# Down products placed between the second-half gate and up products in seven of eleven feed-forward blocks

## What is computed

```
def _swiglu(x, w_in, w_out):
    gate, up = jnp.split(x @ w_in, 2, axis=-1)
    return (jax.nn.silu(gate) * up) @ w_out

x = _layernorm(DEEPNORM_ALPHA * x + FFN_RESIDUAL * _swiglu(x, ffn_w_in[i, f], ffn_w_out[i, f]), ...)
```

## Time and profile before

| what | value |
|---|---|
| time, median of 3 runs | 1402.48 us (1402.14 to 1402.58) |
| the profiled execution | 1402.65 us |
| its span, first to last instruction | 1400.8 us |
| PE busy | 1388.0 us (99%) |
| DVE busy | 1090.6 us (78%) |
| ACT busy | 695.7 us (50%) |
| POOL busy | 61.4 us (4%) |

### The profile page before, as it was taken

The page is one execution under the profiler, slowest core; times in us unless marked ns, Lnnn a source line. Parts: engine busy times, 40 slices in busy tenths (PEclk is TensorE's granted clock), DMA queues, the critical chain, the costliest instruction groups (busy, mean ns, idle before and its releaser), DMA issues.

```text
span 1400.8 us, 21435 instructions
## 1 busy us (share of the span) xinstructions
PE 1388.0 (99%) x8920; PEld 1248.0 (89%) x8920; DVE 1090.6 (78%) x1416; ACT 695.7 (50%) x907; POOL 61.4 (4%) x116
## 2 busy tenths in 40 slices
PE   9999999999999999999999999999999999999997
PEld 8888889999999888888888888899999998888886
DVE  6766687889888986667976667868998889766687
ACT  5544445674546454444454444457646464544442
POOL 0600000000000110000000000000000001000000
PEclk9999999999999999999999999999999999999998
DMA  9765545547654686555566555555466447665541
GB/s 299 248 216 183 197 158 170 188 146 234 205 151 153 199 267 202 180 181 180 181 211 219 190 191 181 180 180 167 154 227 181 151 157 241 213 198 197 189 150 60
DMA packets 169280, 265.31 MB, mean 189 GB/s; under 512 B 9294, under 2 KB 102048, under 8 KB 169184
## 3 DMA queue, kind: packets, MB, share of 16 engines
q1 hardware_dynamic: 163936, 249.53, 54.0%
q0 software_dynamic: 5104, 14.29, 3.5%
q10 hardware_dynamic: 144, 0.13, 0.0%
HBM read 260.51 MB, written 1.05 MB: 187 GB/s over the span
## 4 chain that ended last, share of the span: by engine, by line
PE 97%; DVE 2%; DMA 0%; SPq 0%; ACT 0%; issue 0%; DVEq 0%
PE ps L1593 21%; PE ps L1416 19%; PE ps L1418 19%; PE ps L1417 19%; PE ps L1595 11%; PE ps L1453 4%; PE ps L1715 2%; PE ps L1560 1%; DMA raw<-in_ffn_w_in 0%; DVE big L953 0%; DVE wlo L864 0%; PE ps L1828 0%; DVE xtok L958 0%; PE ps L1576 0%; PE ps L1808 0%; DVE big L988 0%
## 5 line engine op out<-in xcount | busy, mean ns | idle before, releaser
L864 DVE TENSOR_TENSOR wlo<-raw,whi 128x1024 fp32r<-128x1024 f32 x468 | 549.0, 1220 | 159.8 <-ACT whi L587 159.6
L587 ACT CAST whi<-raw 128x1024 fp32r<-128x1024 f32 x460 | 458.8, 1049 | 369.5 <-PE ps L1418 229.9
L1593 PE MATMUL ps<-xhl,whi 128*128 128x512 f32 x1280 | 446.2, 392 | 0.0
L1595 PE MATMUL ps<-xhl,wlo 128*128 128x256 f32 x1280 | 357.9, 280 | 0.0
L1416 PE MATMUL ps<-xhl,whi 128*128 128x256 f32 x1056 | 298.5, 283 | 0.0
L1418 PE MATMUL ps<-xhl,wlo 128*128 128x256 f32 x1056 | 296.3, 281 | 0.0
L1417 PE MATMUL ps<-xhl,whi 128*128 128x256 f32 x1056 | 296.2, 281 | 0.0
L1593 PEld LDWEIGHTS ps<-xhl,whi 128*128 128x128 f32 x1280 | 240.2, 188 | 52.9
L1595 PEld LDWEIGHTS ps<-xhl,wlo 128*128 128x128 f32 x1280 | 240.5, 188 | 1.4
L1416 PEld LDWEIGHTS ps<-xhl,whi 128*128 128x128 f32 x1056 | 199.1, 189 | 2.0 <-issue 1.8
L1417 PEld LDWEIGHTS ps<-xhl,whi 128*128 128x128 f32 x1056 | 199.1, 189 | 0.1
(11 more groups left out here) (267 smaller groups left out, 1430.9 us busy)
## 6 DMA issues: line engine op xcount, KB each, us to landing
raw<-in_ffn_w_in SPq DMA_DIRECT2D x170, 512.0 KB, 5.0
raw<-in_w_in SPq DMA_DIRECT2D x140, 512.0 KB, 4.5
raw<-in_ffn_w_out SPq DMA_DIRECT2D x88, 512.0 KB, 4.1
raw<-in_w_br SPq DMA_DIRECT2D x32, 512.0 KB, 5.0
raw<-in_w_out SPq DMA_DIRECT2D x16, 512.0 KB, 4.6
raw<-in_ple_gate_w SPq DMA_DIRECT2D x16, 512.0 KB, 4.6
gv<-in_ln_g POOLq DMA_DIRECT2D x8, 512.0 KB, 4.5
b_bc<-in_ln_b POOLq DMA_DIRECT2D x8, 512.0 KB, 6.3
```

The source lines that it names most:

```text
L587: nc.scalar.copy(whi[:, slot, half_], raw[:, source, half_]).then_inc(whi_half, 1)
L864: ins = nc.vector.tensor_tensor(low, source_, high.bitcast(F32), ALU.subtract)
L1593: nc.tensor.matmul(ps[:, 2 * q + u, :], w[:, k, u, P * q:P * q + P], xhl[:, :, 4 * kk + k, :], start=kk == 0 and k == 0, stop=False, skip_ ...
L1595: ins = nc.tensor.matmul(ps[:, 2 * q + u, 256:512], v[:, k, u, P * q:P * q + P], xh[:, 4 * kk + k, :], start=False, stop=kk == 1 and k == ...
```

## The change

For j = 2 to 8, `gate_up(j)` also issues the 24 down matmuls of block j-1. They stand in kk = 1: behind each of the last 12 of its 16 pairs come two of them (`down_steps`), in the same order as before. The separate `down(j-1)` calls behind the block fall away. The signals `gate0_done` and `chunk_used` of the block are sent by the last pair of q = 0 and of q = 1, ahead of the two down matmuls that follow there. The first down matmul now waits for `hlo_made` and for its chunk behind the fifth pair of kk = 1.

On ACT and DVE, in the same seven blocks, the cast and the low part of chunk g+5 (= 3j+4, the down chunk of the next step) move from behind `hhi` and `hlo` to between: on ACT ahead of the silu of q = 1, on DVE between `sums` and product of q = 1. No arithmetic and no transfer is added or removed.

```
@@ ACT, ffn @@
+                    woven = 2 <= j < NFF - 2
...
                     else:
+                        if woven:
+                            his(g + RING + 2)
                         act.wait_ge(gsum_made, 2 * (n - n0 // NFF))
                         nc.scalar.activation(sil[:, 1, :], gsum[:, 1, :], ACT.Silu).then_inc(silu_made, 1)
@@ DVE, ffn @@
                             sums(n, q, g)
+                            if q == 1 and 2 <= j < NFF - 2:
+                                los(g + RING + 2)
                             product_of_sums(n, q)
@@ PE, ffn @@
-                def gate_up(j):
+                def gate_up(j, woven=None):
...
+                                    if woven is None or kk == 0:
+                                        continue
+                                    if q == 0 and u == 1 and k == 3:
+                                        ins.then_inc(gate0_done, 1)
+                                    if q == 1 and u == 1 and k == 3:
+                                        ins.then_inc(chunk_used, 1)
+                                    if 8 * q + 4 * u + k >= 4:
+                                        down_steps(woven, 2 * (8 * q + 4 * u + k - 4), 2)
-                            if kk == 1 and q == 0:
+                            if kk == 1 and q == 0 and woven is None:
                                 ins.then_inc(gate0_done, 1)
-                        ins.then_inc(chunk_used, 1)
+                        if woven is None or kk == 0:
+                            ins.then_inc(chunk_used, 1)
...
+                def down_steps(j, first, count):
+                    c = c0 + wo_at(j)
+                    if first == 0:
+                        pe.wait_ge(hlo_made, n0 + j + 1)
+                        chunk_ready(c)
+                    w, v = weights(c, 2, D)
+                    hi, lo = hhi[j % HIDS], hlo[j % HIDS]
+                    for i in range(first, first + count):
+                        t, cg, k, kind = i // 12, i // 6 % 2, i // 3 % 2, i % 3
+                        ins = nc.tensor.matmul(ps[:, 4 + 2 * t + cg, :], (hi, hi, lo)[kind][:, k, P * t:P * t + P],
+                                               (w, v, w)[kind][:, k, W * cg:W * cg + W], start=False, stop=False,
+                                               skip_group_check=True)
+                        if i == 23:
+                            ins.then_inc(chunk_used, 1)
...
                 for j in range(2, NFF - 2):
-                    gate_up(j)
-                    for t in range(TT):
-                        down(j - 1, t)
+                    gate_up(j, woven=j - 1)
```

## The result

The changed kernel takes 1405.39 us (median of 18 runs, 1404.64 to 1405.60) against 1402.50 (18 runs, 1402.13 to 1403.20): a ratio of 1.0020, 95% interval 1.0014 to 1.0027. It is 2.9 us slower. That is 0.01 us within the upper end of the range (1405.4) and just past the line that the forecast drew at 0.2% (1405.3), beyond which it would call the kernel slower, with a chance of 0.14. The single figure of 1403.2 was 2.2 us too low.

What follows compares the result with a forecast made beforehand. The prediction took PE's pace to bound the kernel. Its terms, -0.8 + 0.9 + 0.6 = +0.7 us on the profiled 1402.65, gave 1403.2 against a median of 1402.48; the range was 1400.6 to 1405.4.

Steps and rivals of the forecast that it cites:

- What bounds the kernel: Whole kernel: PE is busy 99% of the span, so the change can give only a better pace, not a saved wait.
- the woven block: Sign to check in the new profile: one woven block again takes 16.69 us, within 0.05.
- the group: Sign to check: a pair and two down matmuls take 0.813 us, off by no more than 0.008.
- The down matmuls' own pace: Woven blocks: three more short threes a block save 0.01 us each, 0.8 us in all; ends nothing and 2.0 us.
- The return: Going from down back to gate matmuls, 11 more times a block: 0.003 us each, 0.9 us; ends 0 and 4.3.
- changing between the two kinds costs more: Slower rival: each of 336 groups of pair and two down matmuls loses over 0.0083 us, up to 1407.4; chance 0.10.
- The faster rival: Weaving takes away all of the down matmuls' extra: -2.0 us with no wait, 1400.6; chance 0.06.
- the tight place: Start of gate_up(10), where DVE's sums were to be done only 0.04 us before PE wants the banks.
- gate_up(10): Behind block 9: PE waits 0.15 us for DVE's sums, four times, 0.6 us in all, between 0 and 2.
- Cover and queues: Woven blocks: `hlo` ready at 5.49, wanted at 7.76, spare 2.3 us; 13.2 us for loads; no new PE wait.
- the head of the line: Slower rival: moved cast and low part hold up the work queued behind them on ACT and DVE; 1408, chance 0.04.
- The clock: PE's granted clock stays full; rival that it falls in places, 16.7 us per woven block at 1.2 GHz, 1420; chance 0.01.

Runs made afterwards that it cites:

- the threes run: Changed kernel, but three down matmuls behind every second pair of the second chunk, 8 groups a block: 1404.09 us, ratio 1.0011.
- fours: Changed kernel, but four down matmuls behind every second pair: 1402.52 us, ratio 1.0000.
- G D g D: Changed kernel, but one down matmul (D) between a pair's 512-column (G) and 256-column (g) matmuls and one behind, last twelve pairs of the second chunk: 1399.97 us, ratio 0.9982.

## Why the prediction was right or wrong

**What bounds the kernel: right.** PE alone; no new wait in 28 woven blocks; the sign and most of the size hang on pace.

**The range: held by luck.** It contains the result by 0.01 us, and its upper end was no sum of terms but a return cost "near its upper part". Of the forecast's own signs, the woven block failed (16.77 us, not 16.69 within 0.05) and the group just held (0.820, not 0.813, off by 0.007 where 0.008 was allowed). Twelve groups at that 0.008 already make 0.1 us a block, so the two signs did not agree with each other.

**The down matmuls' own pace (-0.8 us): wrong.** It rested on the first three of a row being 0.01 us shorter, and took this for an effect of the pair ahead. In the weave the first down matmuls behind a pair are at 0.40 us (64.66, 65.48 in the timeline after), and the threes run shows no saving at all. The term is 0 at best.

**The return (+0.9 us, ends 0 and 4.3): the term that was mis-sized.** The group lost 0.820 - 0.8133 = 0.0067 us, twelve times 0.0067 = 0.080 us a block. The one short three of before is lost too, which about makes up the 0.086 measured. That is 2.4 us, where the two terms together had been put at 0.1. The reason given for the lower end, that the drawn-out matmul stands in the second pair, failed: in the weave the first pair is drawn out too. As a rival ("changing between the two kinds costs more", decided from 0.0083) it came close: measured as 2.4 / 336 = 0.0072 us. But a price per change, which both the term and the rival assumed, does not exist: fours keep half the changes and lose almost nothing, and G D g D doubles them and gains. Two rows cannot carry a price that depends on the order of four.

**The faster rival: its argument did not hold.** It did not come true in this order, as forecast. But it took 0.69 us a three as the least that a down matmul can cost, and asked for less than 0.229 us each, a pace that no row of before has. In the order G D g D a down matmul comes to (0.800 - 0.347) / 2 = 0.227 us. Even so the whole kernel, at 1399.97 us, just misses the forecast's line for faster, 1399.7: the tight place takes 1.3 us back.

**gate_up(10) (+0.6 us, 0 to 2): right in place and mechanism**, 0.08 us instead of 0.15 each, 0.3 us in all. The sums ended at T = 11.44 against a forecast 11.53 (165.71 with T = 0 at 154.27), so 0.13 us ahead of PE was still too little. The run without the moved steps, put at 1407.8, came out at 1408.1.

**Cover and queues: right.** `hlo` at 5.41 against 5.49 forecast and 7.76 wanted; the load and the head of the line cost nothing.

**The clock: right.** It stayed full, 1.00 from 50 to 168 us, with PE busy for all of that stretch. The Trainium skill (TensorE: Matmul & The Clock Gate, "A second HAM failure mode: psum-queue depth-cycling") tells of a kernel in which cycling through banks left PE idle briefly and often, so that its clock fell and rose again. This trace shows neither the idle PE nor the falling clock. Two slips of the forecast change nothing: in the kernel before, the bank changes at every fourth pair (four k per bank), not at every eighth, and a woven block has 12 pairs with twos, not 24.

## What to carry to other kernels

Where an engine is busy all the time, read its pace from start to start for every neighbour that a new order will make. Where the trace of before has no such neighbours, try several orders on the chip: the same 88 matmuls took from 16.55 to 16.78 us here. A weave is worth trying at the finest grain, one matmul of each kind in turn, not only in the order in which the code has them. Shorter blocks uncover the next chain: look at the first block behind the woven stretch, where the old spare time was smallest.

## What was unexpected of the hardware

At the full granted clock (1.00 from 50 to 168 us in every run), with a weight load for each matmul (8920 of either), the pace of PE depended on the order of neighbouring matmuls by up to 2.5% (0.800 against 0.820 us for 1792 columns), without any wait in the woven blocks. It was independent of what ACT and DVE did meanwhile (16.687 and 16.773 us with and without the moved steps), of alternating PSUM banks within a down row, and of which of the three products comes second. The rows of 24 down matmuls ran at 0.233 to 0.234 us each in the four orders that were tried. What in the engine sets this is open: these runs did not vary where the operands lie, nor the widths alone.
